# The first expert load's two waits on output-weight landings taken out of SyncE's program

## What is computed

```python
ada = silu(c) @ w_ada + b_ada                  # six rows of 2048: shift, scale, gate, twice
h = rms_norm(x, g_pre_mix) * (1 + sc_m) + sh_m
y = concat(diff_attention(h), gla(h)) @ w_out  # w_out: 2048 x 2048
x = x + gt_m * rms_norm(y, g_post_mix)
h = rms_norm(x, g_pre_ffn) * (1 + sc_f) + sh_f
combine = top1_group_top2_experts(h)           # 32 experts
y = sum over experts e of combine[e] * ((silu(h @ w1[e]) * (h @ w3[e])) @ w2[e])
out = x + gt_f * rms_norm(y, g_post_ffn)
```

## Time and profile before

| | before |
|---|---|
| median of 3 runs | 1452.66 us (1451.88 to 1452.72) |
| the profiled execution's own time | 1452.2 us |
| its span in the profile | 1450.3 us |
| PE busy | 1221.5 us, 84% of the span |
| VectorE (DVE) busy | 780.4 us, 54% |
| ScalarE (ACT) busy | 210.4 us, 15% |
| bytes moved by DMA | 583.52 MB, mean 402 GB/s |
| chain that ended last | DMA 42%, PE 33%, DVE 3% |

### The profile page before, as it was taken

One profiled execution on the slowest core, in us unless ns is written; L12 is line 12 of the kernel. 1 busy time (PEld: TensorE's weight loads), 2 busy tenths in 40 slices (PEclk: granted clock), 3 DMA queues, 4 the chain that ended last, 5 costly groups with the idle time before them and its releaser, 6 DMA issues.

```text
span 1450.3 us, 18992 instructions
## 1 busy us (share of the span) xinstructions
PE 1221.5 (84%) x7437; PEld 573.8 (40%) x7438; DVE 780.4 (54%) x1106; ACT 210.4 (15%) x489; POOL 53.6 (4%) x76
## 2 busy tenths in 40 slices
PE   4899999999999989877776667767776679999967
PEld 3678788644444443222232222222222223333322
DVE  5777379897888765433343234323332335555525
ACT  3011131223111041000010001000000001111103
POOL 1000300020000020000000000000000000000020
PEclk9999999999999999888788789888888889999989
DMA  9999977999999899999999999999999999999996
GB/s 354 389 389 377 311 294 293 389 374 382 411 411 405 316 390 423 430 431 431 432 432 433 430 432 431 433 431 432 433 431 431 431 433 433 431 432 431 431 427 263
DMA packets 81653, 583.52 MB, mean 402 GB/s; under 512 B 5376, under 2 KB 30256, under 8 KB 56912
## 3 DMA queue, kind: packets, MB, share of 16 engines
q1 hardware_dynamic: 74256, 564.41, 94.4%
q10 hardware_dynamic: 5808, 14.85, 2.7%
q0 software_dynamic: 1552, 3.75, 0.9%
HBM read 579.30 MB, written 3.69 MB: 402 GB/s over the span
## 4 chain that ended last, share of the span: by engine, by line
DMA 42%; PE 33%; DVE 3%; issue 1%; ACT 1%; POOL 0%; SPq 0%; ACTq 0%; DVEq 0%
DMA stream<-in_w 41%; PE ps L1064 9%; PE ps L832 6%; PE ps L1120 4%; PE ps L1071 3%; PE ps L1020 2%; PE ps L923 2%; PE ps L1014 2%; DVE stream L1350 1%; PE ps L928 1%; PE ps L932 1%; DMA stream<-in_w_out 1%; PE ps L1026 0%; PE ps L890 0%; PE ps L900 0%
## 5 line engine op out<-in xcount | busy, mean ns | idle before, releaser
L1064 PE MATMUL ps<-stream,wk 128*32 128x512 f32 x2304 | 330.0, 711 | 178.8 <-DMA stream<-in_w 178.1
L1589 DVE TENSOR_TENSOR acc<-ps,acc 128x2048 f32<-128x2048 f32 x37 | 84.8, 2291 | 359.2 <-PE ps L1020 359.2
L1064 PEld LDWEIGHTS ps<-stream,wk 128*32 128x32 f32 x2304 | 74.7, 125 | 417.3 <-issue 329.9
L1120 PE MATMUL ps<-stream,cst 128*32 128x512 f32 x1152 | 131.5, 595 | 7.8 <-DMA stream<-in_w 7.8
L717 PE MATMUL ps<-stream 128*128 128x256 f32 x512 | 117.0, 388 | 6.3 <-DVE stream L1196 2.1
L832 PE MATMUL ps<-stream 128*128 128x512 f32 x256 | 112.7, 593 | 0.0
L717 PEld LDWEIGHTS ps<-stream 128*128 128x128 f32 x512 | 99.1, 194 | 26.9 <-issue 7.8
L1071 PEld LDWEIGHTS ps<-cst,wk 128*128 128x128 f32 x576 | 77.3, 209 | 69.7 <-issue 69.7
L1020 PE MATMUL ps<-wk,cst 32*128 32x512 f32 x592 | 92.1, 694 | 0.8 <-ACT wk L1929 0.8
L1210 DVE SCALAR_TENSOR_TENSOR wk<-stream,cc,wk 128x768 f32<-128x768 f32 (+1 forms) x90 | 83.5, 928 | 11.2 <-DMA stream<-in_w_ada 8.6
L1071 PE MATMUL ps<-cst,wk 128*128 128x32 f32 x576 | 85.5, 295 | 0.0
(11 more groups left out here) (291 smaller groups left out, 1151.9 us busy)
## 6 DMA issues: line engine op xcount, KB each, us to landing
stream<-in_w SPq DMA_DIRECT2D x87, 4096.0 KB, 41.8
stream<-in_w_ada SPq DMA_DIRECT2D x64, 1024.0 KB, 7.7
stream<-in_w SPq DMA_DIRECT2D x16, 2048.0 KB, 11.5
stream<-in_w_in SPq DMA_DIRECT2D x7, 4096.0 KB, 15.5
stream<-in_w_ada SPq DMA_DIRECT2D x64, 384.0 KB, 9.8
stream<-in_w_ada SPq DMA_DIRECT2D x16, 512.0 KB, 9.7
stream<-in_w_in SPq DMA_DIRECT2D x4, 2048.0 KB, 13.4
stream<-in_w_out SPq DMA_DIRECT2D x2, 4096.0 KB, 17.3
```

Source lines behind the costliest of these rows:

```text
L1064: last = nc.tensor.matmul(bank(1 + m)[32 * g:32 * g + 32, :], xe[:, k + g, :], w13[m][:, k + g, :], start=(k == 0), stop=(k == KD - 4))
L1120: last = nc.tensor.matmul(bank(2)[32 * g:32 * g + 32, :], hid[:, k, :], w2v[:, k, 512 * g:512 * g + 512], start=(k == 0), stop=(k == 3))
L1589: V.tensor_tensor(y4, ps[:, b0:b0 + 4, :], y4, ALU.add).then_inc(ysum_sb, 1)
```

## The change

SP's first load for the experts waits only for the last of the 64 modulation rows to be used. The two waits for the landings of B12 and B22 are taken out. Nothing else in the program differs.

```diff
             sp.wait_ge(ada_done, 64)
-            sp.wait_ge(unit_in[1], 16 * 6)
-            sp.wait_ge(piece_in[0], 16 * HALF_PIECE)
             first_load(1, w3[0])
             sp.wait_ge(proj_ps, FILLS + 8)
             sp.wait_ge(mix_sb, 8)
```

## The result

The changed kernel takes 1461.08 us, the median of 4 runs (1460.57 to 1463.01), against 1452.69 us for the kernel before, measured beside it (4 runs, 1451.88 to 1453.39). The ratio is 1.0059, 95% interval [1.0045, 1.0073]: slower by 8.4 us. 1462.0 was forecast, in a range from 1458.5 to 1465.2.

A forecast was written before the change was run, and what follows sets the result against it. The prediction saw the expert stage as a DMA stream of fixed bytes whose start hangs on B12's landing. 1452.2 us plus 9.7 for B12's delay, other terms zero, gave 1461.9, as a median 1462, range 1458.5 to 1465.2.

The forecast's parts named there:

- Step 1: SP's first expert load: issued at 467.21 us, after the last modulation row, 11.5 us earlier than before.
- Steps 2 and 3: DMA queues q1 and q10: at most 3.5 MB left for B12; packets alternate, so practically the whole load goes ahead.
- The rival of sharing by bytes: DMA queues share by bytes, not packets: B12 7.9 to 8.5 us later, 1460.4 us in total; chance 0.06.
- that of the older transfer keeping its place: DMA engines finish the earlier issue first: B12 lands at 478.7, time stays 1452.2 us; chance 0.06.
- Step 4: B12's landing: delayed by the load's full service time, 4.19 MB in 9.7 us, to 488.4 us.
- The range of 7.9 to 10.9: B12's delay: 7.9 us from sharing by bytes, 10.9 us from the load at q10's own slower rate.
- Step 5: VectorE and ScalarE up to x1: B12's delay passes whole, second half of x1 to 529.9 us, +9.7; PE 7.5 late.
- the rival by which PE sets the pace: ScalarE finds room, so only PE's lateness remains: +7.5 us, 1459.7 us in total; chance 0.05.
- Step 6: SP's later loads and DMA: they neither lengthen nor shorten the shift; the x loads cost nothing.
- Step 7: PE's clock: gaps of 1.4, 2.8 and 3.3 us between products should not lower it; zero, 1 us of range.
- The sum: Whole kernel: profiled execution's 1452.2 us plus 9.7 gives 1461.9 us, as a median 1462.
- The two rules: DMA: issuing early and waiting late gives 1452.2 us; queues served packet by packet gives the prediction's sum.

The follow-up runs named there:

- half the load: Changed kernel with only the first half of the load issued before the two waits, the second half behind them: 1458.59 us, ratio 1.0039.
- the kernel with that order: Changed kernel with ScalarE's reordering of the first half moved behind the last two squares and the four copies after them: 1462.76 us, ratio 1.0069.
- The second comparison: The changed kernel measured once more, unaltered, against the kernel before: 1462.58 us against 1453.7, ratio 1.0065.
- the kernel before with the squares first: Kernel before, with ScalarE's reordering of the first half moved behind the last two squares and four copies: 1455.53 us, ratio 1.0016.

## Why the prediction was right, step by step

**Step 1, the issue time**, was right: 466.31 us, at the end of the last modulation row (456.57 + 9.72 = 466.29).

**Steps 2 and 3, who passes whom**, were right in what matters. Packets alternate (223 to 220, at a size never seen together before), so all of the load is served first. The rival of sharing by bytes and that of the older transfer keeping its place fell with this row and with the kernel that waits for B22 only. Two parts were off. The load's data began about 3.7 us after its issue and not 2.3: q1 had one packet before 470 us. The profile before had shown 2.9: issued at 478.67, first packet at 481.56 us. And the 3.5 MB left on q10 were 2.3: 1131 packets of 2 KB had still to start when the load's first ones did. Neither enters the price here. What counts is the engine that finishes B12 last: it must have as many turns left as the load has packets for it, 16 if they are spread evenly.

**Step 4, the main term**, was sized at 9.7 us. VectorE's idle time grew by 10.15 us in one profile and 9.81 in the other, 4.82 for half the load. The range of 7.9 to 10.9 held it.

**Step 5, the way to x1**, was right. B12's delay went through whole: T1 to the second residual sum takes 41.53 us before and 41.54 after. PE waited as said, 1.20 us for B22's landing before product 2, 2.88 for T1:

```profile
482.45 7.13 PE L963 MATMUL ps<-stream 128*128 128x512 f32 x16 [1.20 <-DMA stream<-in_w_out]
492.47 8.80 PE L963 MATMUL ps<-stream 128*128 128x512 f32 x16 [2.88 <-DVE stream L1348]
502.61 7.11 PE L963 MATMUL ps<-stream 128*128 128x512 f32 x16 [1.34 <-DVE stream L1348]
```

PE ended 2 us ahead of ScalarE; the rival by which PE sets the pace would have needed another order on ScalarE, and the kernel with that order shows the 2 us at the residual sum.

**Step 6, DMA**, was right: no backlog at the first steady load (from 549 to 552 us q1 was busy for 46.1%, 47.4% before), which moved by 9.24 us, the same as the residual sum (9.23). The 4.19 MB loaded earlier bought nothing. That ScalarE's issue of x might be held was right as well, and it cost nothing: the first of the two took 4.37 us instead of 0.35, and ScalarE's next work came at 493.14 us, 13.8 us after the second.

**Step 7, PE's clock, was wrong** in its reason. I had put gaps of up to 3.3 us at zero. Product 3, after a gap of 2.88 us, took 8.80 us instead of 7.1, at a granted clock of 0.60. It cost nothing here only because product 4 waited for T2 anyway, which the step had not counted on: the zero held by luck.

**The sum** says 1461.9 for an execution like the profiled one; it took 1460.65. The missing 1.3 us are +0.45 at the landing, -0.93 ahead of it and -0.84 from the first steady load to the end (908.93 before, 908.09 after): scatter of single profiles, as far as the table shows, and not a gain of the change. The second comparison, 8.9 us, is nearer to the forecast 9.7 than the first.

**The two rules** that the prediction set against each other: the round of the queues, packet by packet (the Trainium skill, *DMA: Bandwidth & Descriptors*, Queues, rings and completion order), agrees with the rows here: where both queues have work their packets alternate (223 to 220, 381 to 376). The advice to issue early and wait late (the Trainium skill, the same page, Rules for kernel authors) did not hold in the changed kernel, where VectorE waited for a transfer on another queue and the time grew by 8.4 us. On B12's own queue the early issue was free (ratio 1.0006).

## What to carry to other kernels

A wait in front of a bulk load can be a reservation of bandwidth for a small transfer that the critical engine waits for. Before taking it out, look at what else is in flight on another queue, in packets and not in bytes: here a load with 16 KB packets passed one with 2 KB packets at 8 to 1 in bytes, and delayed it by its own full service time. A small rest of the critical transfer is no safety: count its packets on the engine that finishes last, where about a dozen turns remained and still cost 8.0 us. If the load must go early, put it behind the critical transfer on the same queue. Packets as small help only when little is left (1.2 us instead of 8.0); with 2.1 MB left they still cost 6.7 us. And look whether the loads queued behind the early one can move too; here they could not, and it gained nothing even where it was free.

## What the hardware showed unexpectedly

PE's granted clock fell after gaps of only 2 to 3 us, but not after each of them. The stages by busy time of the changed kernel (PE, PEld, DVE, ACT, POOL, then PEclk, DMA share, GB/s), around product 3:

```profile
490.00:494.00 4.00, 1.53 (x4) 0.82 (x5) 3.93 (x3) 0.72 (x2) 0.00 (x0) 0.97 0.18 74
494.00:498.00 4.00, 4.00 (x7) 1.59 (x6) 3.84 (x4) 0.00 (x0) 0.00 (x0) 0.60 0.00 0
498.00:502.00 4.00, 3.27 (x8) 1.14 (x6) 3.96 (x2) 0.00 (x0) 0.00 (x0) 1.00 0.00 0
```

PE was idle for most of 490 to 492.5 us; then the clock was mostly at the lower of its two levels (1.2 of 2.4 GHz; 0.60 on average over these 4 us), then full again. The same in the kernel before with the squares first, where PE had waited 1.93 us instead of 1.27, and in the kernel with only B12's wait, where a wait of 1.96 us before unit 10's product was enough. In the run before, a wait of 2.03 us at that place left the clock at 1.00. Before product 3 too, 2.66 us led to 8.60 us of work in the changed kernel's second profile, and 2.67 us to 7.11 us with the squares first. So the length of the gap alone does not decide it. The rows of the two kernels, squares first and only B12's wait:

```profile
534.00:538.00 4.00, 4.00 (x6) 1.40 (x5) 2.76 (x13) 0.00 (x0) 0.00 (x0) 0.58 1.00 426
```

```profile
466.00:470.00 4.00, 2.82 (x4) 1.20 (x5) 1.93 (x3) 0.43 (x1) 0.00 (x0) 0.73 1.05 387
470.00:474.00 4.00, 4.00 (x9) 1.78 (x8) 0.00 (x0) 0.00 (x0) 0.00 (x0) 0.85 1.05 387
```

In both it reached the end of the stage: the filler products of the first took 1.7 us more (4.52 against 2.82), and the first five products of the second took 36.30 us instead of 34.60, so that VectorE waited 0.63 and 1.23 us for PE and the second residual sum came 1.8 us later after T1. The kernel with the load on B12's queue shows the same: a wait of 2.12 us, the clock at 0.65 from 466 to 470 us, 36.25 us. In the changed kernel's second profile the first three products took 22.56 us instead of 20.87, and the later T1 hid it. A gap of 2 us before dense matmuls should be given a price of 0 to 1.8 us here, not zero.
